# Hybrid mLSTM and dilated-attention block: loads of the heads' output at other steps with their sums spread out, w_out's low parts on VectorE, the second convolution a product later, splits of h in another order

## The reference

```
h = rmsnorm(x) * pre_w
proj = h @ w_in      # q,k,v,o,z of the mLSTM (1024 columns each), 8 gates,
                     # q,k,v of the attention (1536 each), z_a (512), g_m, g_a (1024 each)
q_m, k_m = silu(causal_depthwise_conv(q_m, k_m, width 4))
hm = mlstm_chunkwise(q_m, k_m/16, v_m, i, log_f)      # 4 heads of 256, chunks of 128 tokens
hm = rmsnorm_per_head(hm * sigmoid(o_m)) * m_norm_w * silu(z_m)
branch_m = hm @ w_pm
att = 3 groups (window, dilation) of banded softmax attention, merged by their weights
branch_a = (att * silu(z_a)) @ w_pa
merged = sigmoid(g_m) * branch_m + sigmoid(g_a) * branch_a
y = merged @ w_out
return x + rmsnorm(y) * post_w
```

## Time and profile before

| | before |
|---|---|
| runs (us) | 1410.4, 1406.2, 1407.75 |
| median (us) | 1407.75 |
| profiled execution (us) | 1408.32 |
| its span (us) | 1406.5 |
| mean granted clock of PE, share of full speed | 0.985 |
| busy share PE / DVE / ACT / POOL | 97% / 56% / 46% / 41% |
| DMA, mean share of 16 engines | 39.3% on the one queue |

### The profile page before, as it was taken

How to read it: one execution, slowest core, us unless ns; L and a number is a source line. 1 busy time by engine, 2 the same in 40 slices (tenths; PEclk the granted TensorE clock), 3 DMA queues, 4 the chain that set the end, 5 groups by cost and what they waited for, 6 DMA issues and landing times.

```text
span 1406.5 us, 18724 instructions
## 1 busy us (share of the span) xinstructions
PE 1363.8 (97%) x6436; PEld 1133.2 (81%) x6436; DVE 790.5 (56%) x1253; ACT 643.9 (46%) x1321; POOL 582.2 (41%) x408
## 2 busy tenths in 40 slices
PE   7799999999999999999999999999999997999898
PEld 5588888888888888878888888888888886887686
DVE  6755337345543845957666665765543444766532
ACT  6544544543454455345445445444554554334221
POOL 3434345335443534544435344444434552355300
PEclk8999999999999999999999999999999999999899
DMA  6113133323333323463443434434443248856221
GB/s 188 45 42 99 41 74 106 94 51 100 97 83 70 94 65 69 135 185 124 111 141 84 163 124 111 154 94 141 116 149 109 78 159 291 278 164 229 85 91 60
DMA packets 211358, 165.02 MB, mean 117 GB/s; under 512 B 33296, under 2 KB 187440, under 8 KB 211264
## 3 DMA queue, kind: packets, MB, share of 16 engines
q1 hardware_dynamic: 211264, 163.81, 39.3%
HBM read 117.41 MB, written 40.08 MB: 112 GB/s over the span
## 4 chain that ended last, share of the span: by engine, by line
PE 90%; DVE 3%; issue 2%; DMA 2%; ACT 2%; SPq 1%; POOL 0%; DVEq 0%; POOLq 0%; ACTq 0%
PE proj L1207 68%; PE proj L1169 5%; PE proj L1147 2%; PE keep L1252 2%; PE bank L1231 2%; PE keep L1308 2%; PE bank L1317 2%; PE bank L1240 1%; PE bank L1280 1%; PE bank L1313 1%; PE bank L1263 1%; DMA raw<-w_pa 1%; DMA x_sb<-x_in 1%; DVE pm_sb L1720 1%; DMA out_raw<-w_out 1%
## 5 line engine op out<-in xcount | busy, mean ns | idle before, releaser
L1060 POOL TENSOR_TENSOR w_lo<-raw,w_hi 128x512 fp32r<-128x512 f32 x164 | 232.1, 1415 | 447.4 <-ACT w_hi L1409 447.4
L1207 PE MATMUL proj<-hi_T,w_hi 128*128 128x512 f32 x832 | 339.7, 408 | 14.7 <-ACT snap L1427 7.0
L1207 PE MATMUL proj<-hi_T,w_lo 128*128 128x512 f32 x832 | 326.8, 393 | 0.0
L1207 PE MATMUL proj<-lo_T,w_hi 128*128 128x512 f32 x832 | 326.0, 392 | 0.0
L1207 PE MATMUL proj<-hi_B,w_hi 128*128 128x512 f32 x624 | 255.7, 410 | 4.1 <-DVE lo_B L1987 3.9
L1207 PE MATMUL proj<-hi_B,w_lo 128*128 128x512 f32 x624 | 244.9, 392 | 0.0
L1207 PE MATMUL proj<-lo_B,w_hi 128*128 128x512 f32 x624 | 244.5, 392 | 0.0
L1060 POOL TENSOR_TENSOR w_lo<-s_sb,w_hi 128x512 fp32r<-128x512 f32 x104 | 154.3, 1486 | 177.8 <-ACT w_hi L1409 177.5
L1207 PEld LDWEIGHTS proj<-hi_T,w_hi 128*128 128x128 f32 x832 | 157.4, 189 | 49.4 <-issue 12.1
L1207 PEld LDWEIGHTS proj<-hi_T,w_lo 128*128 128x128 f32 x832 | 157.3, 189 | 34.6
L1207 PEld LDWEIGHTS proj<-lo_T,w_hi 128*128 128x128 f32 x832 | 157.7, 190 | 30.6
(11 more groups left out here) (239 smaller groups left out, 2035.5 us busy)
## 6 DMA issues: line engine op xcount, KB each, us to landing
raw<-w_in SPq DMA_DIRECT2D x95, 512.0 KB, 6.0
m_spill<-stage SPq DMA_DIRECT2D x16, 1024.0 KB, 6.1
chunk<-m_spill SPq DMA_DIRECT2D x32, 512.0 KB, 3.7
gate_spill<-stage SPq DMA_DIRECT2D x8, 1024.0 KB, 4.1
gst<-gate_spill SPq DMA_DIRECT2D x32, 256.0 KB, 3.1
share<-share_spill SPq DMA_DIRECT2D x12, 512.0 KB, 4.7
x_sb<-x_in SPq DMA_DIRECT2D x8, 512.0 KB, 6.9
hm_spill<-stage SPq DMA_DIRECT2D x4, 1024.0 KB, 8.9
```

The source lines that it names most:

```text
L1060: TT(w_lo_ring[k % RING][:], src, w_hi_ring[k % RING][:].bitcast(F32), ALU.subtract).then_inc(lo_pool, 1)
L1207: mm = pe.matmul(acc(p, which), w[:, kt, :], m[:, kt, :], start=(first and kt == 0 and w is wh and m is h_hi[b]), stop=(kt == 3 and w is w ...
```

## The change

Four parts, told apart by letters that the text ahead uses too.

**A, the start.** PE transposes the second half of h's columns in the order (0, 4, 1, 5) after step 0 and (2, 6, 3, 7) after step 1, before (0, 4) and (1, 5, 2, 6, 3, 7). DVE makes the first low part before it scales x's tile 5, and POOL waits for all eight scalings ahead of its low part of weights 1. ACT takes T3 and the high parts of weights 5 and 6 ahead of T4, and B22 last. DVE makes sums and lows of T4 ahead of S4, then S4 and the lows of B22.

**B, the second convolution.** j=0 moves by one step, with its taps, tanh and silu; the spill moves to at+17, and `ready` to the next step.

**C, the heads' output.** The loads move to W0 (B11, T1, B22) and W0+2 (B21), behind the loads of the gates in the same step. The sums stand at W0+1 to W0+4 behind the gate product of their step, the high parts one step later, the low parts at W0+3 to W0+8.

**D, the end.** w_out's low parts are DVE's. Its high parts come later. Output tile 0 goes through the rows kt of w_out with both halves of the columns for each, so that it needs a low part every 6 matmuls, before every 3. The last quarter of merged for tile 0 stands in step NK, behind the low parts.

```diff
-        ready = 7 * pair_of["mo", h] + 10
+        ready = 7 * pair_of["mo", h] + 11
...
-            for j, a in ((1, 7), (0, 11)):
+            for j, a in ((1, 7), (0, 12)):
...
-            sp_late[at + 16].append(("spill", p))
+            sp_late[at + 17].append(("spill", p))
...
-    for at, b in ((W0 - 2, "B11"), (W0 - 2, "B21"), (W0 - 1, "T1"), (W0, "B22")):
-        sp_late[at].append(("hm_in", b))
     hm_hi_no, hm_lo_no = {}, {}
-    for at, b in ((0, "B11"), (1, "B21"), (2, "T2"), (2, "T1"), (3, "T3"), (4, "T4"), (5, "B22")):
+    for at, b in ((0, "B11"), (1, "B21"), (3, "T2"), (3, "T1"), (4, "T3"), (5, "T4"), (6, "B22")):
         for i in range(2):
             hm_hi_no[b, i] = len(hm_hi_no) + 1
-            act_late[W0 + at].append(("hm_hi", b, i))
-    for at, b in ((1, "B11"), (2, "B21"), (3, "T2"), (3, "T1"), (4, "T3"), (5, "T4"), (6, "B22")):
-        for i in range(2):
-            hm_lo_no[b, i] = len(hm_lo_no) + 1
-            dve_late[W0 + at].append(("hm_lo", b, i))
-    for at, b in ((0, "T1"), (0, "T2"), (0, "T3"), (1, "T4")):
-        for i in range(2):
-            dve_late[W0 + at].insert(i + 2 * ("T1", "T2", "T3", "T4").index(b) if at == 0 else i, ("hm_sum", b, i))
+            act_late[W0 + 1 + at].append(("hm_hi", b, i))
+    for at, b, i in ((1, "T1", 0), (1, "T1", 1), (2, "T2", 0), (2, "T2", 1), (2, "T3", 0), (3, "T3", 1),
+                     (4, "T4", 0), (4, "T4", 1)):
+        dve_late[W0 + at].append(("hm_sum", b, i))
+    for at, b, i in ((3, "B11", 0), (3, "B11", 1), (4, "B21", 0), (5, "B21", 1), (5, "T2", 0), (5, "T2", 1),
+                     (6, "T1", 0), (6, "T1", 1), (6, "T3", 0), (7, "T3", 1), (7, "T4", 0), (7, "T4", 1),
+                     (8, "B22", 0), (8, "B22", 1)):
+        hm_lo_no[b, i] = len(hm_lo_no) + 1
+        dve_late[W0 + at].append(("hm_lo", b, i))
     for t in range(KT):
         sp_late[W0 - 1 if t < 2 else W0 if t < 4 else W0 + t - 1].append(("gate_in", t))
         sp_late[W0 + t + 2].append(("pa_out", t))
+    for at, b in ((0, "B11"), (0, "T1"), (0, "B22"), (2, "B21")):
+        sp_late[W0 + at].append(("hm_in", b))
...
-            act_late[at + 2].append(("out_hi", i, j))
-            pool_late[at + 2].append(("out_lo", i, j))
+            act_late[min(at + 4, NK)].append(("out_hi", i, j))
+            dve_late[(at + 4, NK - 1, NK, NK)[i]].append(("out_lo", i, j))
     sp_late[NK - 1].append(("post_in",))
     act_late[NK - 2].append(("merged_hi", 0, 0))
     dve_late[NK - 2].append(("merged_lo", 0, 0))
+    act_late[NK].append(("merged_hi", 0, 1))
+    dve_late[NK].append(("merged_lo", 0, 1))
...
+
+            g.wait_ge(x_norm, NT)
             low(1)
...
+                def rows_of_w_out(kt, half):
+                    i, j, columns = kt // 2, kt % 2, half_of(half)
+                    for a, w in ((hi_part, out_hi), (hi_part, out_lo), (lo_part, out_hi)):
+                        mm = pe.matmul(y_slot(t)[:, columns], a[:, kt, :], w[i][:, j, columns],
+                                       start=(kt == 0 and a is hi_part and w is out_hi),
+                                       stop=(kt == KT - 1 and a is lo_part))
+                    return mm
+
+                if t == 0:
+                    for kt in range(KT):
+                        if kt == 6:
+                            pe.wait_ge(mg_lo, 2)
+                        pe.wait_ge(w_out_lo, kt + 1)
+                        for half in range(2):
+                            mm = rows_of_w_out(kt, half)
+                            if kt == KT - 1:
+                                mm.then_inc(pe_y, 1)
+                    return
                 for half in range(2):
-                    columns = half_of(half)
                     for kt in range(KT):
-                        if t < 2 and kt == 6:
-                            pe.wait_ge(mg_lo, 2 * t + 2)
-                        i, j = kt // 2, kt % 2
-                        if t == 0:
-                            pe.wait_ge(w_out_lo, kt + 1)
-                        for a, w in ((hi_part, out_hi), (hi_part, out_lo), (lo_part, out_hi)):
-                            mm = pe.matmul(y_slot(t)[:, columns], a[:, kt, :], w[i][:, j, columns],
-                                           start=(kt == 0 and a is hi_part and w is out_hi),
-                                           stop=(kt == KT - 1 and a is lo_part))
+                        if t == 1 and kt == 6:
+                            pe.wait_ge(mg_lo, 4)
+                        mm = rows_of_w_out(kt, half)
                     mm.then_inc(pe_y, 1)
...
-                for kt in {0: (0, 4), 1: (1, 5, 2, 6, 3, 7)}.get(k, ()):
+                for kt in {0: (0, 4, 1, 5), 1: (2, 6, 3, 7)}.get(k, ()):
...
-            for j in range(4):
-                second_half(j)
-                h_high("T2", j, 2 * j + 2)
-                if j == 0:
-                    after(0)
-                elif j == 1:
-                    high(2)
-                    high(3)
+            second_half(0)
+            second_half(1)
+            h_high("T2", 0, 2)
+            after(0)
+            second_half(2)
+            h_high("T2", 1, 4)
+            high(2)
+            second_half(3)
+            h_high("T2", 2, 6)
+            high(3)
+            h_high("T2", 3, 8)
             for j in range(4):
                 h_high("T1", j, 2 * j + 1)
             high(4)
+            after(2)
             for j in range(4):
-                if j == 2:
-                    after(2)
                 h_high("T3", j, 9 + j)
             high(5)
-            for j in range(4):
-                h_high("B22", j, 8)
+            high(6)
             after(4)
             for j in range(4):
                 h_high("T4", j, 13 + j)
-            high(6)
+            for j in range(4):
+                h_high("B22", j, 8)
...
+                elif what == "out_lo":
+                    i, j = it[1:]
+                    dve.wait_ge(w_out_hi, 2 * i + j + 1)
+                    TT(out_lo[i][:, j, :], out_raw[i][:, j, :], out_hi[i][:, j, :].bitcast(F32), ALU.subtract
+                       ).then_inc(w_out_lo, 1)
...
             scale(4)
+            first_low(0)
             scale(5)
-            first_low(0)
...
             sums_and_low("T3", third_sum, 8)
+            sums_and_low("T4", fourth_sum, 12)
             add(0, "S4")
-            sums_and_low("T4", fourth_sum, 16)
             for j in range(4):
-                h_low("B22", j, 12 + j + 1, h_ready["B22"])
+                h_low("B22", j, 16 + j + 1, h_ready["B22"])
```

More of the change, by code:

```diff
@@ L615, in hybrid_kernel @@
         pa_done, gated, mg_done, mg_lo = sem("pa_done"), sem("gated"), sem("mg_done"), sem("mg_lo")
+        w_out_lo = sem("w_out_lo")
         y_ms, y_read, y_done = sem("y_ms"), sem("y_read"), sem("y_done")
@@ L621, in hybrid_kernel @@
         lo_pool = sem("lo_pool")
-        m_rs, w_out_lo, y_rs = sem("m_rs"), sem("w_out_lo"), sem("y_rs")
+        m_rs, y_rs = sem("m_rs"), sem("y_rs")
         block = ctx.enter_context(nc.Block())
@@ L1103, in _ @@
                         TT(mrs[:], msq[:, h % 2], halfneg[:], ALU.pow).then_inc(m_rs, 1)
-                    elif what == "out_lo":
-                        i, j = it[1:]
-                        g.wait_ge(w_out_hi, 2 * i + j + 1)
-                        TT(out_lo[i][:, j, :], out_raw[i][:, j, :], out_hi[i][:, j, :].bitcast(F32), ALU.subtract
-                           ).then_inc(w_out_lo, 1)
             for t in range(NT):
@@ L1688, in _ @@
                     piece(it)
-            merged_high(0, 1)
             for part in range(2):
@@ L2182, in result @@
                         ALU.mult, ALU.add).then_inc(y_done, 1)
-            merged_low(0, 1)
             for part in range(2):
```

## The result

The changed kernel takes 1400.6 us (median of 4 runs, 1399.3 to 1402.1) against 1408.3 before (median of 4 runs, 1406.2 to 1410.4; a fourth run, of 1408.9, was added to the three of the table above); the ratio is 0.9945, with a 95% interval of 0.9926 to 0.9965. So it is 7.7 us faster. The forecast was 20.0 us faster (1388.3), with a range up to 1398: the sign was right, the size was not, and the measured time lies outside the range.

A forecast was written before the change was run, and what follows sets the result against it. PE, the matrix engine, 97% busy, was taken as the bound. Gains of 7.2 + 6.3 + 8.9 + 10.2 = 32.6 us less 12.6 lost gave 20.0: 1408.3 to 1388.3 us, range 1374 to 1398.

The forecast's parts named there:

- A: Start: reordered ACT and DVE work removes PE's 3.86 us wait and its slow matmuls; 7.2 us gained.
- B: Second convolution a step later: PE's 3.9 us wait for ACT's copy near 600 us goes; 6.3 us gained.
- B': Each head's first chunk, loaded behind a weight pair, makes PE wait: 10.2 us plus 2.4, 12.6 us lost.
- The clock's price: After a long PE wait, twelve matmuls run at 1.2 GHz, costing 2.4 us more; charged once for the four first chunks.
- C: Heads' output: the 7.8 us PE wait before PA2 and its slow matmuls go, PA3 loses 0.7; 8.9 us gained.
- D: End: w_out's low parts on DVE, tile 0 starts earlier and waits less; 10.2 us gained, bounds 7 and 11.3.
- Rival 1: The heads' first chunks land in time, so B' loses nothing; 1375.7 us, chance 0.18.
- Rival 2: One large term fails: at the start or in C another wait replaces the removed one; 1396 us, chance 0.18.

## Why the prediction was wrong

**A** was right in its main step, 0.8 us too high (7.2, measured 6.4 in this pair of traces, 5.7 alone). P3 began at 63.47, where "it can't begin before 62.8". As forecast, POOL's wait of 3.86 is gone with its slow stretch, and the first product starts 0.8 us later, at 19.66. The wait of 2.3 us for ACT's copy is gone too, but one of 2.0 us for DVE's low part stands in its place. That the term is so near is in part luck: the same start came 4.3 to 6.6 us early in eight traces.

**B** was right: 6.3, measured 6.4.

**B'** failed in the step "I take the price for one, 2.4, as the two stand right at the border". What the first chunks wait for was right, and the waits were near in sum (10.2, measured 11.7). The first head's was 3.5 and not 2.2, as SP also waited 1.2 us for a spill to land before it could issue the chunk, which the sum didn't have. The clock's price was mis-sized: three waits had a slow stretch behind them, and these cost 2.8, 1.7 and 3.1 us beside the waits, 7.9 with the 0.3 at the second head. Matmuls in the wait took 6.6 of it away. The prediction took the price for a matter of length, with a border between 2.3 and 3.4 us; the runs showed no such border. A wait of 3.5 us at the first head cost 2.8 us more in the changed kernel and 0.3 with part C put back. What they support is 2.0 us on the mean for each of the three long waits, which from the rows gives 11.7 + 6.0 + 0.3 = 18.0 for the term. The lower bound was mis-added as well: "all four with a slow stretch" is 10.2 + 4 x 2.4 = 19.8 and not 16.

**C** failed in leaving out the end of the stage; the bounds "5 (T1 at 1189, two more waits in PA4 and PA5)" look only for waits up to PA5. T1 itself came as forecast: 1185.0 in the old trace's time is 1192.0 here, where the stage lies 7.0 us later, and the sums started at 1191.8; PA3 waited 0.3 us, 0.7 was the forecast. Up to the end of P1 the gain was still 7.6 us. From there to the end of P6 of the first w_pm pair 4.5 us were lost: the wait of P2 for PA7's gate product, 2.6 us idle, and the slow matmuls behind it. I followed DVE's list only to PA3, though its rows showed that the low parts had been spread out to the last step, and never asked what P1 and P2 wait for. Adding up the list at the 1.18 us of the prediction wouldn't have shown the wait either: 27 of them and one of 0.7 us, from 1191.8 on, end at 1224.4, ahead of P2. The other half of the miss is that six of them took 2.31 us beside POOL. The prediction had this effect in D and left it out here. The runs showed that late loads aren't the cause (the wait stays without them), and that another order on DVE is enough to take the wait away. That keeping POOL's work apart from DVE's would do it too is only worked out from the rows; no run did it.

**D** was right: 10.2, measured 10.7, with the last product ending where it was put (1306.2 here, 3.8 us later than 1302.3 by the shift) and one wait of 0.5 us in tile 0, where 1.1 was the forecast.

Rival 1 (the first chunks in time) is true only with another order on the queue, and then at 1382.7 and not 1375.7, as C's loss is in it. Rival 2 (one large term fails) came true for C, but B' failed at the same time by more: 5.7 and 7.0 us, both of the same sign, are what put the time out of the range. Either of them alone would have left it inside.

## What to carry to other kernels

Price a wait of the matrix engine together with the slow stretch that can follow it, and give that price a mean and a range from many waits, not a border from two; here it was 0.3 to 3.1 us, 2.0 on the mean, for waits of 3.1 to 4.0 us. A sum of four such waits has a far wider range than its parts. When work is spread out over a stage, add up the engine's list to the stage's last consumer, not only to the first one that gains, and with the longer time of the instructions that run beside another engine's. And when a load has to go a step later, look at what is issued first in that step: where a transfer is urgent, it belongs ahead of the bulky one.

## What was not expected of the hardware

The length of the idle time alone doesn't tell whether the clock falls. After waits of 2.3 us it stood at 1.00 in the kernel before (48.50 to 51.20), after 2.6 us at 0.50 here. Behind the same wait of 2.0 us near 46 us it stayed at 1.00 in the changed kernel, and with the first chunk ahead of the pair it fell to 0.51 about 1.3 us later. In the kernel before, it also fell about 1 us after a wait of 1.9 us (the tile's first matmul at 1305.75), 7 us after another wait of 2.3 us; with tile 0 by rows alone, which has the same two waits, it didn't. In the changed kernel, waits of 3.1, 3.5 and 4.0 us cost 3.1, 2.8 and 1.7 us more: the longest has the shortest slow stretch behind it. And two executions ran at a mean clock of 0.94 to 0.95, one with matmuls in its waits and one (three low parts behind PA7's gate product) without any, so those matmuls aren't needed for it. Why the clock does so, these runs don't tell.
